# A transposed triangular inverse made by unit-matrix products and ACT copies instead of masked products and DVE copies

## The reference

```python
A = jnp.where(strict, jnp.einsum('bnhid,bnhjd->bnhij', kb, k) * gamma, 0.0)
eye = jnp.eye(C, dtype=jnp.float32)
T = lax.linalg.triangular_solve(A + eye, jnp.broadcast_to(eye, A.shape), left_side=True, lower=True, unit_diagonal=True)
u = T @ (v * beta[..., None])
w = T @ (kb * jnp.exp(g)[..., None])
```

## Time and profile before

| what | value |
|---|---|
| median of 3 runs | 2023.73 us (2020.12 to 2024.34) |
| the profiled execution | 2028.97 us, of it the span of its instructions 2027.2 us |
| PE matmul busy | 1810.3 us (89%), 18321 instructions |
| DVE busy | 539.6 us (27%), 1218 instructions |
| ACT busy | 295.8 us (15%), 639 instructions |
| mean granted TensorE clock | 0.936 |

### The profile page before, as it was taken

How to read it: one execution, slowest core, us unless ns; L and a number is a source line. 1 busy time by engine, 2 the same in 40 slices (tenths; PEclk the granted TensorE clock), 3 DMA queues, 4 the chain that set the end, 5 groups by cost and what they waited for, 6 DMA issues and landing times. The chain is left out here.

```text
span 2027.2 us, 40308 instructions
## 1 busy us (share of the span) xinstructions
PE 1810.3 (89%) x18321; PEld 1429.0 (70%) x18321; DVE 539.6 (27%) x1218; ACT 295.8 (15%) x639; POOL 72.0 (4%) x109
## 2 busy tenths in 40 slices
PE   5797687889999899877778799999999999999996
PEld 3685576777888777766667444558985898579853
DVE  4435666532000156365553100000000000000002
ACT  2012332200000024222220100100010001000101
POOL 0001321100000000010000000000000000000000
PEclk8899798989999999888878799999999999999998
DMA  9618642204334053000000797899999999999993
GB/s 369 278 42 374 250 168 85 85 10 166 143 148 166 23 237 125 6 12 12 12 7 1 297 399 286 353 428 426 426 415 427 426 424 418 428 427 426 409 428 157
DMA packets 37132, 492.54 MB, mean 243 GB/s; under 512 B 4379, under 2 KB 4540, under 8 KB 7452
## 3 DMA queue, kind: packets, MB, share of 16 engines
q1 hardware_dynamic: 36956, 489.90, 58.9%
HBM read 487.53 MB, written 2.36 MB: 242 GB/s over the span
## 5 line engine op out<-in xcount | busy, mean ns | idle before, releaser
L2054 PE MATMUL bank<-ring,arena 128*32 128x128 f32 x2016 | 227.6, 273 | 0.0
L2051 PE MATMUL bank<-ring,arena 128*32 128x384 f32 x2016 | 224.8, 487 | 2.2 <-DMA ring<-in_experts 2.2
L2054 PEld LDWEIGHTS bank<-ring,arena 128*32 128x32 f32 x2016 | 217.9, 110 | 0.0
L2046 PE MATMUL bank<-ring,arena 128*64 128x256 f32 x1792 | 204.8, 381 | 3.2 <-DMA ring<-in_experts 3.2
L2046 PEld LDWEIGHTS bank<-ring,arena 128*64 128x64 f32 x1792 | 126.2, 137 | 80.7 <-issue 22.4
L2248 DVE TENSOR_TENSOR arena<-bank,arena 128x256 f32<-128x256 f32 (+2 forms) x56 | 28.5, 508 | 549.0 <-PE bank L2054 155.0
L1343 PE MATMUL bank<-arena,ring 128*128 128x256 f32 x704 | 155.6, 383 | 3.8 <-DVE arena L303 3.8
L1343 PEld LDWEIGHTS bank<-arena,ring 128*128 128x128 f32 x704 | 134.9, 192 | 23.6 <-issue 4.1
L2204 ACT ACTIVATE arena<-bank 128x256 f32<-128x256 f32 (+2 forms) x56 | 25.3, 451 | 699.7 <-PE bank L2054 294.1
L1464 PE MATMUL bank<-arena,ring 128*128 128x256 f32 x512 | 115.9, 389 | 6.1 <-DVE arena L303 3.8
L1464 PEld LDWEIGHTS bank<-arena,ring 128*128 128x128 f32 x512 | 99.7, 196 | 23.8 <-issue 5.8
(11 more groups left out here) (391 smaller groups left out, 2275.8 us busy)
## 6 DMA issues: line engine op xcount, KB each, us to landing
ring<-in_experts SPq DMA_DIRECT2D x168, 2048.0 KB, 20.7
ring<-in_stream SPq DMA_DIRECT2D x61, 2048.0 KB, 11.3
xT<-in_xT SPq DMA_DIRECT2D x1, 1024.0 KB, 6.9
arena<-in_s0gd SPq DMA_DIRECT2D x4, 256.0 KB, 3.4
out_sgd<-arena SPq DMA_DIRECT2D x4, 256.0 KB, 2.5
out_y<-arena SPq DMA_DIRECT2D x4, 256.0 KB, 2.5
arena<-in_masks SPq DMA_DIRECT2D x1, 832.0 KB, 4.5
arena<-in_hfw SPq DMA_DIRECT2D x1, 544.0 KB
```

The costliest lines, as they stand in the source:

```text
L2046: mm = nc.tensor.matmul(out[HALF * x:HALF * x + HALF, 0:256], h[:, j, 0:HALF], w[:, j, 256 * x:256 * x + 256], start=start, stop=stop, til ...
L2051: nc.tensor.matmul(out[lo:hi, 0:3 * P], h[:, j, lo:hi], w[:, j, 0:3 * P], start=start, stop=stop, tile_position=(0, lo), skip_group_check= ...
L2054: mm = nc.tensor.matmul(out[MID:P, r * P:(r + 1) * P], h[:, j, 32 * r:32 * r + 32], w[:, j, 3 * P:4 * P], start=(start and r == 0), stop=s ...
```

## The change

The second product for U (line 737) and DVE's predicated copy into U (line 756) go, and with them the semaphore `s_XU`. In their place the new `pe_transposes` multiplies T, as the stationary operand, with the unit matrix, eight products of 64 x 64 into bank 2 + g, and the new `act_transposed` copies the bank whole into U. From level 2 on this is done within the level, from T of the level before: on PE behind the first products of the same batch, on ACT behind the copy of X. At level 1 U is that of `dve_first`, so nothing is added there. At level 5 both batches have the second product into T; U of batch 0 is then made from the finished T by a last unit-matrix product and copy, which stand behind the level on PE and on ACT and ahead of the solution. The counts on the semaphores follow, and two waits are added at the start of a pair in the RWKV block. The number of banks is as before.

```diff
--- before.py
+++ after.py
@@ -680,9 +680,8 @@
 
 
         s_id, s_T, s_U = ([sem(f"{n}{g}") for g in range(2)] for n in ("identity_set", "T_level_done", "U_level_done"))
-        s_X, s_Xs, s_TX, s_XU = ([sem(f"{n}{g}") for g in range(2)] for n in ("AT_done", "AT_copied", "TAT_done", "TATt_done"))
-        NT, NU = (LEVELS - 1, LEVELS), (LEVELS, LEVELS - 1)
-        NTX, NXU = (LEVELS - 2, LEVELS - 1), (LEVELS - 1, LEVELS - 2)
+        s_X, s_Xs, s_TX, s_Tt = ([sem(f"{n}{g}") for g in range(2)] for n in ("AT_done", "AT_copied", "TAT_done", "T_transposed"))
+        NU, NTt = (LEVELS, LEVELS - 1), (LEVELS - 1, LEVELS - 2)
 
         blk = lambda h: slice(HB64 * h, HB64 * h + HB64)
         s_Z, s_Zs = ([sem(f"{n}{g}") for g in range(2)] for n in ("solved", "solution_copied"))
@@ -714,47 +713,57 @@
                         ins = nc.vector.copy_predicated(dst[rows], self.level_mask(upper, 0, rows), part)
                     ins.then_inc(done, 1)
 
+            def pe_transposes(self, pe, r, l, g):
+
+                pe.wait_ge(s_T[g], r * LEVELS + l)
+                pe.wait_ge(s_U[g], r * NU[g] + l - 1)
+                for q in range(4):
+                    for h in range(2):
+                        mm = nc.tensor.matmul(ps[2 + g][blk(h), q * HB64:(q + 1) * HB64], self.T[g][blk(h), q], ident[blk(h), blk(h)], start=True, stop=True,
+                                                 tile_position=(HB64 * h, HB64 * h))
+                mm.then_inc(s_Tt[g], 1)
+
             def pe_level(self, pe, r, l, up):
                 for g in range(2):
-                    pe.wait_ge(s_T[g], r * NT[g] + l)
+                    pe.wait_ge(s_T[g], r * LEVELS + l)
                     for q in range(4):
                         for h in range(2):
                             mm = nc.tensor.matmul(ps[g][blk(h), q * HB64:(q + 1) * HB64], up(g, q, h), self.T[g][blk(h), q],
                                                   start=True, stop=True, tile_position=(HB64 * h, HB64 * h))
                     mm.then_inc(s_X[g], 1)
+                    if l >= 2:
+                        self.pe_transposes(pe, r, l, g)
                 for g in range(2):
                     pe.wait_ge(s_U[g], r * NU[g] + l)
                     pe.wait_ge(s_Xs[g], r * (LEVELS - 1) + l)
-                    if l < LEVELS - 1 or g == 1:
-                        for q in range(4):
-                            for h in range(2):
-                                mm = nc.tensor.matmul(ps[g][blk(h), q * HB64:(q + 1) * HB64], self.U[g][blk(h), q],
-                                                      self.X[g][blk(h), q], start=True, stop=True, tile_position=(HB64 * h, HB64 * h))
-                        mm.then_inc(s_TX[g], 1)
-                    if l < LEVELS - 1 or g == 0:
-                        for q in range(4):
-                            for h in range(2):
-                                mm = nc.tensor.matmul(ps[2 + g][blk(h), q * HB64:(q + 1) * HB64], self.X[g][blk(h), q],
-                                                      self.U[g][blk(h), q], start=True, stop=True, tile_position=(HB64 * h, HB64 * h))
-                        mm.then_inc(s_XU[g], 1)
+                    for q in range(4):
+                        for h in range(2):
+                            mm = nc.tensor.matmul(ps[g][blk(h), q * HB64:(q + 1) * HB64], self.U[g][blk(h), q],
+                                                  self.X[g][blk(h), q], start=True, stop=True, tile_position=(HB64 * h, HB64 * h))
+                    mm.then_inc(s_TX[g], 1)
+                if l == LEVELS - 1:
+                    self.pe_transposes(pe, r, LEVELS, 0)
+
+            def act_transposed(self, act, r, l, g):
+                act.wait_ge(s_Tt[g], r * NTt[g] + l - 1)
+                act.wait_ge(s_TX[g], r * (LEVELS - 1) + l - 1)
+                nc.scalar.activation(self.U[g].rearrange("p q t -> p (q t)"), ps[2 + g][:, 0:4 * HB64], ACT.Copy).then_inc(s_U[g], 1)
 
             def act_level(self, act, r, l):
                 for g in range(2):
                     act.wait_ge(s_X[g], r * (LEVELS - 1) + l)
                     nc.scalar.activation(self.X[g].rearrange("p q t -> p (q t)"), ps[g][:, 0:4 * HB64], ACT.Copy).then_inc(s_Xs[g], 1)
+                    if l >= 2:
+                        self.act_transposed(act, r, l, g)
+                if l == LEVELS - 1:
+                    self.act_transposed(act, r, LEVELS, 0)
 
             def dve_level(self, dve, r, l):
                 for g in range(2):
-                    if l < LEVELS - 1 or g == 1:
-                        dve.wait_ge(s_TX[g], r * NTX[g] + l)
-                        dve.wait_ge(s_T[g], r * NT[g] + l)
-                        nc.vector.copy_predicated(self.T[g], self.level_mask(0, l),
-                                                  ps[g][:, 0:4 * HB64].rearrange("p (q t) -> p q t", q=4)).then_inc(s_T[g], 1)
-                    if l < LEVELS - 1 or g == 0:
-                        dve.wait_ge(s_XU[g], r * NXU[g] + l)
-                        dve.wait_ge(s_U[g], r * NU[g] + l)
-                        nc.vector.copy_predicated(self.U[g], self.level_mask(1, l),
-                                                  ps[2 + g][:, 0:4 * HB64].rearrange("p (q t) -> p q t", q=4)).then_inc(s_U[g], 1)
+                    dve.wait_ge(s_TX[g], r * (LEVELS - 1) + l)
+                    dve.wait_ge(s_T[g], r * LEVELS + l)
+                    nc.vector.copy_predicated(self.T[g], self.level_mask(0, l),
+                                              ps[g][:, 0:4 * HB64].rearrange("p (q t) -> p q t", q=4)).then_inc(s_T[g], 1)
 
             def pe_solve(self, pe, r, rhs, rhs_ready, lower):
 
@@ -1018,6 +1027,8 @@
                 lora_products(0)
                 for c in range(RWC):
                     if c:
+                        pe.wait_ge(s_T[1], c * LEVELS)
+                        pe.wait_ge(s_U[0], c * NU[0])
                         pe.wait_ge(s_U[1], c * NU[1])
                         pe.wait_ge(s_Ys, c)
                         pe.wait_ge(s_bons, c)
@@ -1651,7 +1662,7 @@
                     if i:
                         inv.solved(pe, RWC + i)
                         pe.wait_ge(s_U[1], (RWC + i) * NU[1])
-                        pe.wait_ge(s_T[1], (RWC + i) * NT[1])
+                        pe.wait_ge(s_T[1], (RWC + i) * LEVELS)
                         pe.wait_ge(s_U[0], (RWC + i) * NU[0])
                     for hh in range(2):
                         h = 2 * i + hh
```

## The result

The changed kernel takes 2029.6 us (median of 8 runs, 2026.1 to 2032.0) beside 2021.05 us for the kernel before in the same comparison: a ratio of 1.0041 with a 95% interval of 1.0026 to 1.0056, that is +8.3 us (5.3 to 11.3). A second set of runs gave 1.0052 (1.0034 to 1.0070). The forecast was +6.7: inside the first interval, and 0.2 under the lower end of the second (+6.9 to +14.2). That the time itself, 2030.4, is met within 1 us is partly luck: the kernel before came out at 2021.05 here, 2.7 under the 2023.73 to which I had added, and the change cost some 2 us more than I had put. The sign is the one that had the larger chance. The profiled execution has a span of 2029.0 us.

The account below looks back on a forecast made before the run. DeltaNet is ruled by waits between engines, a middle level by PE's issue plus one ACT round; 0 - 7.5 + 14.6 - 1.2 + 0.8 = +6.7 us on 2023.73 gives 2030.4 us, range 2022 to 2038.

Parts of the forecast that it names:

- Levels 2 to 4: Middle levels of each inversion: PE's wait only moves, next level starts at 3.12 instead of 3.11 us; 0 in sum.
- Rival B: Levels 2 to 4: DVE's copies were the bound, halving them gains 7.0 us, giving 2023.4 us; chance 0.18.
- Level 1: First level of each inversion: two PE groups go, 0.94 us less in all eight, -7.5 us.
- The sigmoids: Level 2 in three RWKV pairs, copies queued behind four sigmoids: level 3 starts 0.39 us earlier, -1.2 us.
- The end: Level 5 into the solution: last transpose and copy uncovered, +1.91 us in seven pairs, +1.2 in one, +14.6 us.
- The root: RWKV c = 1 and 2: ACT's table load behind U's copy delays the solution's copy, 0.4 us twice, +0.8 us.
- C: DeltaNet level 1 and output stages: clock rises earlier and stays up, sum -4.9 us, 2018.8 us; chance 0.12.
- D: Output stages: PE's new idle time puts the other four on the lower clock, +6.5 us, 2036.9 us; chance 0.14.

Follow-up runs that it names:

- the first experiment: Kernel before with only the last transpose and ACT's copy into U of batch 0 added behind level 5: ratio 1.0081 to before, +16.4 us.

## Why the prediction was right, point by point

**Levels 2 to 4: zero, and it was.** (Level 2 is told with level 1, below.) Level 3 changed by -0.4 and level 4 by -1.7 over eight inversions; with the +2.3 of level 2 the three levels make +0.2, inside the ends of -7.0 and +2.4. A plain level is 3.10 where it was 3.11. Most of the -1.7 is the clock's: level 4 of i = 2 took 4.59 at a granted clock of 0.63 before and 3.10 at 1.00 after, that of i = 1 4.14 at 0.65 and 4.64 at 0.63. These rows also show that I read too much into the one level: I wrote that 3.1 us stands wherever no other work of the pair does, but level 4 of i = 1 to 3 has no such work and took 4.1 to 4.6 before, at the lower clock level for most of it. That DVE's and PE's ends meet (3.10 and 3.12) was my reason that nothing could be gained, and the run with DVE copying U shows the same 3.10 with another engine in the copy's place.

**Rival B falls.** The Trainium skill, TensorEngine Tiling (Array Packing), Performance Considerations, names the copies out of PSUM as a possible bottleneck after a fourfold speed-up by tiling, and would share them between ScalarE and VectorE. The products of the levels use two tiles at a time (the `tile_position` in the diff takes two values), short of that condition. Two copies on each engine (this change), or four on DVE and two on ACT (before, and the run in which DVE copies U): the plain level is 3.09 to 3.11 in each. No run here shows the copies as the bound; where a copy costs, it is for its place in an engine's order.

**Level 1: the right total from two wrong halves.** I took two groups at the upper clock level, 0.94, in all eight. Level 1 gave -10.6 where I had put -7.5, and level 2 +2.3 where I had put -1.2. The traces show 0.60 to 0.62 in c = 0 and 1 where both kernels ran at the upper level (4.00, in the third trace, to 3.40; 4.01 to 3.39), the lower end that I had given: batch 1 waits for its copy of X. In the DeltaNet pairs it was 1.4 to 1.7 (5.95 to 4.37 in i = 0, 6.08 to 4.38 in i = 2). In three of these level 2 gave back 0.6 to 0.9, as part of the lower clock stretch moved into it: that is the mechanism that I had named for taking 0.94. The sigmoids gave -0.4 in c = 0 and c = 2, as worked out, and nothing in c = 1. Together levels 1 and 2 gave -8.3 against -8.7: the nearness is luck in part, and 1.0 of the -8.3 is the step of c = 0 that two of the three traces of before have and the third has not.

**The end: +14.1 against +14.6.** The chain was right link by link, and the eight terms were 1.78 to 1.84, 1.10 in c = 0, and 2.17 in i = 3 (where the end took 4.60, at the lower clock level for a part of it). In all but the last it was 0.1 less than I had put: I let PE go on 0.15 after ACT's copy, and it went on 0.05 after it (893.30 + 0.38 = 893.68, then 893.73). The two runs that add and remove the last transpose alone give 9.33 and 9.66. The first is what it costs on top of the old kernel, the second what it costs in the new one, where level 5 has the transposes as well; those are the other 4.5 of the 14.1.

**The root: +1.3 against +0.8.** I had put it between 0 and 0.72 for each of two pairs and took 0.4. It was 0.66 each: from the solution's start to the output products 4.75 instead of 4.09 in c = 1 and in c = 2. The chain of the table load is the one that I gave. The mis-sized step is that batch 1 would end later anyway and hide nearly half: the second products came 0.84 later (2.05 for 1.21), and only 0.18 of that was taken up before the output. The Trainium skill, ScalarE: Activation LUTs, What ACT_TABLE_LOAD costs, adds some 1.38 us of drain to a load of 1.28. The changed kernel shows the load alone: the root starts 0.01 after its end (361.53, after 360.24 + 1.28), and ACT's copy follows it by 0.38.

**The clock, rivals C and D.** Both happened, in part and against each other. Of the four DeltaNet output stages two (i = 1 and 3) were at the lower level in every trace of before; in both of the changed kernel only i = 3 was. The output stage of i = 1 ran at the upper clock level in both traces of the changed kernel and at the lower one in all three of before (-1.63), and that of c = 1 the other way round. In windows of the changed kernel, the output of i = 1 and then a piece of that of c = 1 (columns as above):

```profile
950.98:953.93 2.95, 2.95 (x26) 2.95 (x27) 0.00 (x0) 0.00 (x0) 0.00 (x0) 1.00 0.00 0
309.00:311.50 2.50, 2.50 (x26) 2.50 (x24) 0.87 (x4) 0.00 (x0) 0.00 (x0) 0.61 0.00 0
```

The first answers the earlier trace rows, where the same products took 4.58 at 0.63; in the second PE is at 0.61, where the kernel before is at 1.00 in the like place. Summed over the three stages between the DeltaNet inversions the change is -1.6, over those of RWKV +2.2 with the root in it, so -0.8 without the root. C and D would have needed four steps of one sign.

**What stays open.** The traces account for 4.2 us in the changed stretches and 5.4 in all, the medians for 8.3 and 10.5, with lower ends of 5.3 and 6.9. Three and two profiled executions, out of kernels whose times spread over 14 us (before, 2014.6 to 2028.5) and 10 us (changed, 2026.1 to 2035.6), don't settle the other 3 to 5. The two blocks differ in this. From its first inversion to its last solution the DeltaNet took 172.73 to 172.81 in the three traces of before and 173.34 and 173.35 in the changed ones: +0.6, clock steps included, each time. The RWKV block took 171.94, 174.38 and 169.00 before and 175.56 and 175.35 changed, so anything from +1 to +6.6. The third trace of before, 2022.55 us, is the only one near the medians, and against it alone the spans differ by 9.6. So the forecast's terms are borne out one by one, and the size of the whole only within some us; what sets the clock's steps in the RWKV block stays open.

## What to carry to other kernels

Replacing one engine's work by another's changes nothing while each has room. Ask of every step of the new scheme whether it stands beside other work or alone, and look at the end of the chain first: here the way from the last level into the solution cost 14 us, more than all that was won, and 9.7 of them are one transpose with its copy, alone on the path eight times. The same idea pays where it stops short of that end: with transposes at levels 2 and 3 alone, and the masked products back from level 3 on, the kernel is 0.4% faster than before instead of 0.4 to 0.5% slower. Part of its price, three inversions of eight, falls into a wait of PE for DVE's normalisation that is there anyway. And of a cost that depends on the clock level, price both levels; a gain at the front of a lower stretch may only move that stretch.

## What the runs showed of the hardware

Not expected: in one block the clock's steps repeat, in the other they don't. The four DeltaNet inversions took 87.88, 87.78 and 87.86 us in three executions of the kernel before, and 90.03 and 90.05 in two of the changed one; the run with the root ahead, which has the same DeltaNet instructions, has 90.07. Level by level they agree within 0.06, at lower and upper clock alike, though the executions start the block up to 6 us apart. In the RWKV block, level 1 of c = 0 took 5.53, 5.52 and 4.00 in the kernel before, and 3.40 and 3.39 in the changed one, but 4.58 in the run with the root ahead, at a granted clock of 0.63 (233.38 to 237.96) where the changed kernel has 1.00, with the same instructions up to there. What a kernel looks like in one trace is thus no sure guide to which of its steps are fixed. Two executions of the changed kernel, which agree to 0.02 us over all eight inversions, would have hidden this.

In the first experiment PE stands idle 0.7 us longer ahead of each solution (3.61 less five groups of 0.47, where it was 2.45 less four). One level 1 and one output stage that had run at the upper clock level in all three traces of before ran at the lower one, and a change costed at 10 to 11 us took 16. That this idle time is what moved them is not shown: it was traced once, and the level 1 lies in the block whose steps come and go.
